# Attention inputs of the last three token tiles made between the expert gathers in a decoder block

## The reference, cut to what matters

```python
q = (rms_norm(c_q, q_a_norm) @ w_uq).reshape(bsz, seq, N_HEADS, QK_HEAD_DIM)      # 256 -> 8 x 96
kv = (rms_norm(c_kv, kv_a_norm) @ w_ukv).reshape(bsz, seq, N_HEADS, QK_NOPE_DIM + V_HEAD_DIM)  # 128 -> 8 x (64 + 64)
k_nope, v = kv[..., :QK_NOPE_DIM], kv[..., QK_NOPE_DIM:]
k = jnp.concatenate([k_nope, k_rope], axis=-1)                # k_rope is shared by the heads, 32 wide
q, k = rms_norm(q, q_norm), rms_norm(k, k_norm)               # then rope on the last 32 of each
# causal attention in blocks of 128 queries, output projection, residual, second norm -> h2
u = expert_down[idx]                                          # idx: (128, 8, 16) per tile
a = jax.nn.gelu(jnp.einsum('thkd,td->thk', u, hc))
y = jnp.einsum('thk,thkd->td', g * a, expert_up[idx])
```

## Time and profile before

| | us |
|---|---|
| timed runs | 3043.6, 3046.6, 3048.8 (median 3046.6) |
| profiled execution | 3042.9, its span 3041.0 |
| `phase_d`, first to last query copy (L1059) | 240.1 to 284.6, then its tail |
| first instruction of `phase_ef` | 295.6 |
| first gather issued, first dot | 357.7, 364.3 |
| last dot starts | 3029.6 |
| bytes moved | 1152 MB, of them 1076 MB by the gathers |

### The profile page before, as it was taken

The page is one execution under the profiler, slowest core; times in us unless marked ns, Lnnn a source line. Parts: engine busy times, 40 slices in busy tenths (PEclk is TensorE's granted clock), DMA queues, the critical chain, the costliest instruction groups (busy, mean ns, idle before and its releaser), DMA issues.

```text
span 3041.0 us, 38212 instructions
## 1 busy us (share of the span) xinstructions
PE 2305.3 (76%) x13074; PEld 1893.3 (62%) x13074; DVE 2213.8 (73%) x5241; ACT 2032.4 (67%) x3757; POOL 1285.3 (42%) x1164
## 2 busy tenths in 40 slices
PE   8998889888878966776677676767667777666766
PEld 4765577777765656665566666666566666555655
DVE  7896678899965967777777666677776666777644
ACT  4234268898866756776667666776776677666665
POOL 1003144344534644444454444444544444444543
PEclk9998999899989967776766777776677767777766
DMA  6252399999999999999999999999999999999998
GB/s 232 41 200 86 148 381 417 403 396 420 420 416 403 397 418 421 421 421 420 420 419 409 421 419 418 406 421 421 421 415 421 420 419 411 422 420 413 417 421 338
DMA packets 174835, 1152.07 MB, mean 379 GB/s; under 512 B 23472, under 2 KB 25392, under 8 KB 43440
## 3 DMA queue, kind: packets, MB, share of 16 engines
q0 software_dynamic: 147984, 1075.90, 85.7%
q1 hardware_dynamic: 26656, 73.72, 6.7%
HBM read 1142.60 MB, written 5.77 MB: 378 GB/s over the span
## 4 chain that ended last, share of the span: by engine, by line
DMA 36%; DVE 21%; PE 16%; ACT 10%; issue 5%; POOL 2%; POOLq 0%; DVEq 0%
DMA pair<-in_experts_dram,idx_g 35%; DVE pair L1918 11%; PE acc_a L1539 5%; ACT pair L1695 5%; PE pef L1514 3%; PE acc_b L1539 3%; POOL pair L1368 2%; PE acc_b L1462 1%; ACT w L1693 1%; ACT L1691 1%; PE turns L1478 1%; ACT L1686 1%; ACT ga L1691 1%; DVE top_i L1846 1%; DVE staged L1847 1%
## 5 line engine op out<-in xcount | busy, mean ns | idle before, releaser
L1368 POOL DMA_INDIRECT pair<-in_experts_dram,idx_g x1024 | 1223.1, 1194 | 1436.6 <-PE acc_a L1539 796.8
L1918 DVE SCALAR_TENSOR_TENSOR pair<-pair,h 128x1024 f32<-128x1024 f32 x1024 | 1247.8, 1221 | 641.5 <-DMA pair<-in_experts_dram,idx_g 626.0
L1695 ACT ACTIVATE pair<-pair,w 128x1024 f32<-128x1024 f32 x1024 | 1176.4, 1149 | 33.3
L1539 PE MATMUL acc_a<-ident,pair 128*128 128x128 f32 x5120 | 850.5, 326 | 365.8 <-ACT pair L1695 355.8
L1539 PEld LDWEIGHTS acc_a<-ident,pair 128*128 128x128 f32 x5120 | 719.7, 169 | 487.8 <-ACT pair L1695 454.1
L1539 PE MATMUL acc_b<-ident,pair 128*128 128x128 f32 x3072 | 595.7, 362 | 282.9 <-ACT pair L1695 278.2
L1539 PEld LDWEIGHTS acc_b<-ident,pair 128*128 128x128 f32 x3072 | 491.1, 188 | 381.0 <-ACT pair L1695 370.8
L1691 ACT ACTIVATE ga<-a 128x1 f32<-128x1 f32 x1024 | 204.1, 199 | 642.3 <-DVE pair L1918 614.0
L1693 ACT ACTIVATE w<-ga,g 128x1 f32<-128x1 f32 x1024 | 301.6, 295 | 33.2
L1514 PE MATMUL pef<-h2t,wq 128*128 128x128 f32 x1536 | 202.1, 296 | 6.3 <-DMA wq<-in_w_query_t_dram 6.3
L1514 PEld LDWEIGHTS pef<-h2t,wq 128*128 128x128 f32 x1536 | 200.6, 214 | 6.7 <-issue 6.7
(11 more groups left out here) (374 smaller groups left out, 2269.4 us busy)
## 6 DMA issues: line engine op xcount, KB each, us to landing
pair<-in_experts_dram,idx_g POOLq DMA_INDIRECT x1024
wrow<-in_w_ada_t_dram SPq DMA_DIRECT2D x12, 1024.0 KB, 6.4
pieces<-in_w_query_t_dram SPq DMA_DIRECT2D x18, 512.0 KB
wada<-in_w_ada_t_dram SPq DMA_DIRECT2D x16, 512.0 KB, 9.7
wq<-in_w_query_t_dram SPq DMA_DIRECT2D x4, 2048.0 KB, 29.1
out_dram<-h SPq DMA_DIRECT2D x8, 512.0 KB
wout_b<-in_w_out_dram SPq DMA_DIRECT2D x1, 4096.0 KB, 33.6
x<-in_x_dram SPq DMA_DIRECT2D x7, 512.0 KB, 15.2
```

What stands on the lines that cost most here:

```text
L1368: p.indirect_dma_start(pair[n % R], None, A["experts"], bass.IndirectOffsetOnAxis(ap=idx[:, t % (2 * PH), k:k + 1], axis=0)).then_inc(pair ...
L1539: last = t.matmul(accs[ACC[i]][:, k * P:(k + 1) * P], pair[n % R][:, D + k * P:D + (k + 1) * P], S.ident[:], is_transpose=True, start=n % ...
L1695: s_.activation(pair[n % R][:, D:], pair[n % R][:, D:], ACT.Copy, scale=w[:, n % NA:n % NA + 1]).then_inc(scaled, 1)
L1918: v.scalar_tensor_tensor(down, down, 1.0, h2[:, n // P, :], ALU.mult, ALU.mult, accum_out=a[:, n % NA:n % NA + 1]).then_inc(dotted, 1)
```

## The change

`phase_d` makes only token tiles 0 to 4 (`HERE = 5`), so its loop runs 6 times. In passes 1 to 3 ScalarE also copies the latent inputs of tiles 5 to 7 to `ct_late`, and GpSimd keeps their rotary tables.

Tiles 5 to 7 are made in `phase_ef`, in six units of four heads. A unit starts at slot `LATE_U[u]` and goes through the single bank `qs`, which the query products of the experts leave free between slots 65 and about 215: key-value product, its read by ScalarE, query product, copy by VectorE, key transposes, query transposes. GpSimd computes the roots and the rotary part between gathers. `wuq` and `wukv` are loaded again, where the query pieces lay, after the ninth query product. `x_load(6)` moves behind the load of `wout_b`. Several tables change by a few slots; `finish` writes to `h2` in place of `gated`; some semaphores are merged.

```diff
-            for it in range(NT + 1):
+            for it in range(HERE + 1):
...
+                if 1 <= i <= NT - HERE:
+                    s.activation(S.ct_late[i - 1][:], S.ct[:, :, tile(HERE + i - 1)], ACT.Copy)
...
-    ASKED_AT = [5, 13, 24, 32, 43, 52, 61, 215, 228, 254, 272, 282, 294, 306, 318]
-    FOUND_AT = [15, 22, 35, 41, 54, 62, 77, 98, 108, 121, 136, 153, 165, 176, 222, 234, 258, 279, 289, 301, 313, 325]
+    ASKED_AT = [5, 12, 22, 29, 38, 49, 60, 215, 231, 255, 261, 282, 294, 306, 318]
+    FOUND_AT = [15, 24, 32, 39, 49, 62, 77, 97, 111, 125, 151, 165, 176, 185, 228, 243, 259, 265, 289, 301, 313, 325]
...
-    STRIDE = lambda t: [1, 1, 1, 2, 1, 2, 2, 1, 2, 2, 2, 2, 2, 1, 2, 2, 1, 1, 1, 1, 1, 1][t - 2] if 2 <= t < 3 * PH else 1
+    STRIDE = lambda t: [1, 1, 1, 1, 2, 1, 2, 1, 2, 2, 2, 2, 1, 2, 1, 2, 1, 1, 1, 1, 1, 1][t - 2] if 2 <= t < 3 * PH else 1
...
+    LATE_U = [65, 75, 86, 100, 112, 126]
+    KV_AT = {n: u for u, n in enumerate(LATE_U)}
+    Q_AT = {n + 2: u for u, n in enumerate(LATE_U)}
+    KT_AT = {n + 7: u for u, n in enumerate(LATE_U)}
+    QT_AT = {n + 9: u for u, n in enumerate(LATE_U)}
+    KV_OUT = {n + 1: u for u, n in enumerate(LATE_U)}
+    K_SUM = {n + 3: u for u, n in enumerate(LATE_U)}
+    Q_OUT = {n + 4: u for u, n in enumerate(LATE_U)}
...
             sp.wait_ge(q_done, PH + 1)
-            x_load(6)
+            sp.wait_ge(s_done, PH)
+            sp.dma_start(wuq_late[:], A["w_uq"][0].rearrange("(k p) n -> p k n", p=P)).then_inc(weights_in, 16)
+            for n in range(2):
+                sp.dma_start(wukv_late[n][:], A["w_ukv"][0][:, 512 * n:512 * (n + 1)]).then_inc(weights_in, 16)
...
+            def root_k(u):
+                i, part_ = unit(u)
+                pool.wait_ge(late_summed, 5 * u + 1)
+                own.step(p.tensor_scalar(ss_late[:], ss_late[:], 1.0 / DQK, S.kss_late[:, i - HERE:i - HERE + 1], ALU.mult, ALU.add))
+                p.tensor_tensor(ss_late[:], ss_late[:], neghalf[:, 0:4], ALU.pow).then_inc(late_rooted, 1)
...
+            def root_q(u):
+                i, part_ = unit(u)
+                pool.wait_ge(late_summed, 5 * u + 3)
...
+                for m, x in enumerate((x1, x2, x2, x1)):
+                    own.mark(p.tensor_tensor(rt[m], x, bcast(S.tab_late[:, m, i - HERE, :], 1, [P, 4, HALF]), ALU.mult))
...
             for n in range(SLOTS):
...
+                if n - 8 in K_ROOT:
+                    root_k(K_ROOT[n - 8])
+                if n - 8 in Q_ROOT:
+                    root_q(Q_ROOT[n - 8])
...
+            def late_kv(u):
+                i, part_ = unit(u)
+                if u == 0:
+                    pe.wait_ge(weights_in, 64)
+                    pe.wait_ge(s_out, PH + 1)
+                else:
+                    pe.wait_ge(late_read, 3 * u)
+                t.matmul(qs[:], S.ct_late[i - HERE][:, 2], wukv_late[part_][:], start=True, stop=True).then_inc(late_made, 1)
...
+            def late_kv_out(u):
...
+                s_.activation(sq_late[:, 0:4 * DN].rearrange("p (h n) -> p h n", h=4), kv[:, :, 0:DN], ACT.Square)
+                s_.activation(kf_late[:, :, 0:DN], kv[:, :, 0:DN], ACT.Copy)
+                s_.activation(S.v[:, i, 256 * part_:256 * (part_ + 1)].rearrange("p (h n) -> p h n", h=4), kv[:, :, DN:], ACT.Copy).then_inc(late_read, 1)
```

204 lines of the change are left out of this document (166 added, 38 removed).

## The result

| | before | changed |
|---|---|---|
| median of the timed runs, us | 3047.2 (20 runs, 3043.6 to 3050.5) | 3051.3 (20 runs, 3046.3 to 3062.7) |
| span of the profiled execution | 3041.0 | 3050.2 |
| first gather issued | 357.7 | 339.2 |

The ratio is 1.0015, with a 95% interval of 1.0009 to 1.0021: by this ratio the change costs 4.6 us and brings nothing. The forecast was 8 us the other way. In code lines the changed kernel has the gather at L1442, the dot at L2065, the scaling at L1834, the add-up at L1615. A unit's steps are L1635 and L1641 on TensorE (products), L1761 to L1763 and L1768 on ScalarE, L2081, L2086, L2090, L2095 and L2100 on VectorE, and L1394 to L1414 on GpSimd.

A forecast was written before the change was run, and what follows sets the result against it. Bytes were taken to bound most of the gather loop, the engines slots 65 to 136, with `phase_d` standing ahead of the gathers. -19.6 + 0.3 + 5.8 + 1 + 4 + 0.5 = -8.0 us, from 3046.6 to 3038.6; 8-in-10 range 3029 to 3052.

The forecast's parts named there:

- Three passes fewer, -19.6 us: `phase_d`: three passes of 6.54 us removed, so everything behind, first gather included, comes 19.6 us earlier.
- 338.5 was the sign and 341 the limit: First gather: expected near 338.5 us; later than 341 us would show the prediction wrong.
- the change doesn't do what it says: Rival: something else ends `phase_d`'s shadow, first gather only some 3 us earlier, 3055 us; chance 0.05.
- Early slots, +0.5: Third query product, moved from slot 13 to 12, delays one add-up and gather 20: 0.5 us, within 0 to 2.5.
- The tables, 0 within 2: Other table shifts of one to fifteen slots move searches within reach of their deadlines: 0, within 2 us either way.
- nothing moves behind slot 176: Loop behind slot 176: only bytes count, both kernels stay at the same distance; a lead changing over 3 us is wrong.
- TensorE's wait for the weights, 7 to 8 us: Slot 65: loads take 13 to 14.7 us, TensorE arrives after 6.3; wait priced at 3 us, bounds 0 and 8.4.
- the DMA queue doesn't run dry: During the weight wait at slot 65, some five outstanding gathers, 12 us of transfer, keep the queue supplied.
- VectorE, 16 us of work, +1 and +5.8: Six units' VectorE work, 16 us: slots 65 to 96 grow by 1 us, slots 96 to 136 by 5.8.
- GpSimd, 30 us of work at a price of 0: Units' roots and rotary part on GpSimd: some 5 us a unit, 30 us; no cost term, busy 52 of 104 us.
- GpSimd in the way: Rival: GpSimd held up by dots, nearly 8 us a unit, late gathers cost 15 us, 3054 us; chance 0.10.
- Given back: Rival: VectorE stays at 96% (+8.2), slots 65 to 96 grow by 3, weight wait counts fully, 3048 us; chance 0.20.

The follow-up runs named there:

- tables_alone: Kernel before with only the moved tables and pitch 8.6 for tile 7; no units, no weight loads, eight tiles in `phase_d`: 3045.5 us, ratio 1.0000.
- no_units: Changed kernel without its six units, tiles 5 to 7 reading earlier tiles' data; short `phase_d`, tables and weight loads stay: 3030.2 us, ratio 0.9943.
- resident: Changed kernel with units multiplying by data already in SBUF, so TensorE doesn't wait for the weights; loads still run: 3048.4 us, ratio 1.0004.
- vectore_alone: no_units plus VectorE's five operations a unit at their slots, waiting for no other engine: 3038.3 us, ratio 0.9972.
- gpsimd_alone: no_units plus GpSimd's 12 operations a unit at their slots, on scratch tiles, with no waits for other engines: 3040.7 us, ratio 0.9977.
- no_roots: Changed kernel without GpSimd's roots and rotary products in the units, but for one product of the keys: 3042.5 us, ratio 0.9990.
- gpsimd_spread: gpsimd_alone with each unit's operations cut into pieces, one per slot over six slots between gathers: 3042.4 us, ratio 0.9980.
- gpsimd_memset: gpsimd_alone with its operations replaced by 17 fills a unit, which read nothing, of about the same total time: 3045.1 us, ratio 0.9992.
- spread_k_on_act: Changed kernel plus early_product, GpSimd's work spread, query norms once a tile, key transposes moved from VectorE to ScalarE a slot earlier: 3040.4 us, ratio 0.9977.
- early_product: Changed kernel with the ninth query product asked for at slot 56 instead of 60, so the weight loads start earlier: 3051.0 us, ratio 1.0007.

## Why the prediction failed

**Three passes fewer, -19.6 us: right.** The passes of `phase_d` start at the same distance as in the earlier trace rows:

```profile
253.72 0.66 DVE L1067 COPY qs<-pdd 128x480 f32<-128x480 f32 x1
260.26 0.66 DVE L1067 COPY qs<-pdd 128x480 f32<-128x480 f32 x1
```

The first gather is issued at

```profile
339.23 2.19 POOL L1442 DMA_INDIRECT pair<-in_experts_dram,idx_g  x1 [22.46 <-DVE idx_g L2034]
```

where 338.5 was the sign and 341 the limit. One trace is not that sharp: with the same `phase_d` it came at 337.1 to 342.3 us in the experiments, and at 360.7 in tables_alone, where before had 357.7. no_units with -17.4 confirms, within 4 us, that the gain reaches the end. This rules out the rival that the change doesn't do what it says.

**Early slots, +0.5: not contradicted.** The lead fell from 18.2 to 17.2 over the first 65 slots, less than the 6 us by which traces of nearly the same first 65 slots differ.

**The tables, 0 within 2: right in sum.** tables_alone has ratio 1.0000. But the sign "nothing moves behind slot 176" failed: slots 192 to 250 take 161.6 us instead of 158.2. The units don't do it, since no_units has 162.4. The moved tables alone have 159.7, less than half of it; the rest stays open.

**TensorE's wait for the weights, 7 to 8 us: 10.6.** TensorE needed 7.3 us from the product's end (534.8) to L1635, where 6.3 were taken; but the loads arrived 18 us behind that end, at 552.8, where 13 to 14.7 were worked out from the earlier trace rows. The DMA issues between 520 and 560 us have

```profile
wuq_late<-in_w_uq_dram SPq DMA_DIRECT2D x1, 768.0 KB, 11.4
wukv_late<-in_w_ukv_dram SPq DMA_DIRECT2D x2, 256.0 KB, 15.5
```

each from its own issue. So the rate that the loads got beside the gathers was taken too large: the earlier trace rows are from a stretch with a DMA share of 0.87, and these loads met one of 1.01 to 1.02; the page of the kernel before has 15.2 us from issue to landing as the median of its seven loads of 0.5 MB of `x`. The step "the DMA queue doesn't run dry" failed too: the rate was 203 GB/s from 555 to 560 us. What the wait costs in the end, taken at 3 within 0 and 8.4, is about 3 by `resident` (ratios 1.0015 and 1.0004, each good to 2 or 3 us); since its reason, a queue that doesn't run dry, failed, that size is in part luck.

**VectorE, 16 us of work, +1 and +5.8: about right in size, and the rule behind it did not hold.** VectorE's operations had the durations worked out from the earlier trace rows:

```profile
L2090 DVE TENSOR_REDUCE by_head<-sq_late 128x4 f32<-128x384 f32 x6 | 3.3, 551 | 3.1 <-ACT sq_late L1768 3.1
L2081 DVE TENSOR_REDUCE ss_late<-sq_late 128x4 f32<-128x256 f32 x6 | 2.5, 412 | 8.1 <-ACT v L1763 8.1
```

(551 and 412 ns, forecast 0.55 and 0.42.) Alone they cost 8.8 us, where 6.8 were priced. But the rule behind it, that VectorE runs 98% full and the stretch takes 109.9 us, did not hold: VectorE was busy 107.6 of 118 us, 91%. vectore_alone, with 5.2 us more than no_units in slots 96 to 136 and VectorE 95% full there, nearly has the priced 5.8. In the changed kernel VectorE has room left, so its own work alone no longer sets the pace. The 13.3 us by which slots 96 to 136 grew hold 4.4 us that the moved tables alone show; the prediction counted the search parts there, found 18 in both kernels and saw no shift.

**GpSimd, 30 us of work at a price of 0: the step that failed.** It was priced at 0 because the engine was busy 52 of 104 us. The work is 48 us, not 30: the roots over four columns took 1.20 and 1.43 us where 1.0 was taken from the earlier trace rows, the products of 64 columns 0.39 to 0.79 us where 0.3 was, and the small ones 0.37 to 0.73 us where 0.23 was, since they stretch under a dot, as the one in the earlier trace rows had shown. And it costs: 10.4 us by gpsimd_alone, 7.6 by no_roots, 7 to 10 in all. The rival named this engine and its sign, and its nearly 8 us a unit are what was measured (it counted 60 operations for 6 units; there are 12 in each, 72). But it put the cost at 15 us and gave it 0.10, and nothing bears out its mechanism, a block that outlasts the lead of the gathers: gpsimd_spread costs the same with the blocks cut up, and by gpsimd_memset shared reads are not needed for the cost. Its chance should have been about that of the forecast, since the earlier trace rows also has the rate at 395 and 409 GB/s with VectorE's 83% and 96% full: a rate under its best in a ring that no one engine fills.

So 3051.3 is the forecast of 3038.6, plus 10 for GpSimd and 2 for VectorE's real price, within 1 us; the prices themselves are good to some 5 us, so the closeness is luck. Two rivals had better numbers by terms that the runs don't show. "GpSimd in the way" was 3 us off at 3054, with a cost of 15 us for this engine. "Given back" was 3 us off at 3048, with VectorE at 96% and the weight wait in full.

**What stays open.** The last link is argued and not shown: that a ring of 8 buffers, in which TensorE, VectorE and ScalarE are all 79 to 91% full, turns each engine's added time into a quarter to a half of itself. Measured are the rates: 10.4 of 41 us for GpSimd, 8.8 of 16 us for VectorE, 15 of 43 us for fills; but 6 of 4.4 us for the operation that spread_k_on_act moved does not fit it. What TensorE's clock has to do with it is open as well: in slots 96 to 136 it is 0.84 to 0.89 in gpsimd_alone, gpsimd_spread, gpsimd_memset, vectore_alone and early_product, and 0.97 in no_units, no_roots and spread_k_on_act. Why fills cost a little more than the mixed operations, and why early_product gives back in slots 96 to 136 half of what it wins in 65 to 96, is not explained by any run here.

## What to carry over

An engine's mean idle time is no cover for new work when it stands in the ring that hands buffers round: do not price it at nothing where the rate of transfer is already below its best; in this loop it cost a quarter to about a third of its duration. Add small operations up with the durations they have in the loop under the other engines' work, not with those of quiet stretches. Before moving work from a quiet prologue into a full loop, test it with the work left out and with each engine's part alone; here the parts added up within what the measurements can tell, and showed that work on the fullest engine was worth taking elsewhere. Compare TensorE's granted clock between such runs too, before their difference is put down to one engine.
